# Norm roots moved behind the products: query, key and last-gate rows of a two-block network on one core

## The reference, cut to what matters

```
# h: 256 x 1024 after the state-space mixer
h = h + sigmoid(rms_norm(h, ple_norm[0]) @ gate_w[0]) * (p[0] @ proj_w[0])
k, v = split(rms_norm(h, kv_norm) @ kv_w)            # 256 + 256 columns
k = rope(rms_norm(k per head of 64, k_norm))
q, gate = split(rms_norm(h, attn_norm) @ in_w)       # 1024 + 1024 columns
q = rope(rms_norm(q per head of 64, q_norm))
h = h + (attention(q, k, v, window 128, sinks) * silu(gate)) @ out_w
h = h + sigmoid(rms_norm(h, ple_norm[1]) @ gate_w[1]) * (p[1] @ proj_w[1])
rms_norm(x, w) = x / sqrt(mean(x*x) + 1e-6) * w
```

## Time and profile before

| | |
|---|---|
| median of 3 runs | 924.22 us (922.49 to 926.22) |
| the profiled execution, its own time | 927.82 us |
| its span in the profile | 926.0 us |
| PE busy | 887.0 us (96%) |
| DVE busy | 667.6 us (72%) |
| ACT busy | 512.7 us (55%) |
| TensorE clock granted, mean | 0.988 of full speed |

### The profile page before, as it was taken

One profiled execution on the slowest core, in us unless ns is written; L12 is line 12 of the kernel. 1 busy time (PEld: TensorE's weight loads), 2 busy tenths in 40 slices (PEclk: granted clock), 3 DMA queues, 4 the chain that ended last, 5 costly groups with the idle time before them and its releaser, 6 DMA issues.

```text
span 926.0 us, 13925 instructions
## 1 busy us (share of the span) xinstructions
PE 887.0 (96%) x5463; PEld 771.8 (83%) x5463; DVE 667.6 (72%) x971; ACT 512.7 (55%) x742; POOL 73.4 (8%) x79
## 2 busy tenths in 40 slices
PE   6999899899999989999999899999999998999998
PEld 6997788788888779999988699988888886878777
DVE  6688648928677688888844687796786777776665
ACT  6865424235453566666534565854756566576553
POOL 6001213100000000000000000007220000000000
PEclk9999999999999999999999999999999998999999
DMA  9542242124554466556555356544223444522231
GB/s 303 173 137 92 92 119 91 46 90 154 196 176 148 170 211 199 183 190 202 201 181 182 104 175 196 169 137 137 92 92 107 178 159 155 197 92 91 92 120 62
DMA packets 80977, 136.37 MB, mean 147 GB/s; under 512 B 3957, under 2 KB 46545, under 8 KB 80912
## 3 DMA queue, kind: packets, MB, share of 16 engines
q1 hardware_dynamic: 78800, 130.95, 43.0%
q0 software_dynamic: 2112, 4.53, 1.8%
HBM read 134.42 MB, written 1.05 MB: 146 GB/s over the span
## 4 chain that ended last, share of the span: by engine, by line
PE 66%; ACT 5%; DVE 5%; issue 3%; DMA 2%; DVEq 0%; ACTq 0%
PE bank L449 19%; PE bank L450 18%; PE bank L451 18%; PE bank L438 3%; DVE lower L1930 2%; ACT upper L1345 1%; PE bank L1124 1%; PE bank L929 1%; PE bank L937 1%; DMA loaded<-in_ssm_in_w 1%; PE bank L1108 1%; ACT arena L1444 1%; ACT arena L1846 1%; DMA loaded<-in_ple_gate_w 1%; DMA loaded<-in_ffn_w_up 1%
## 5 line engine op out<-in xcount | busy, mean ns | idle before, releaser
L1930 DVE TENSOR_TENSOR lower<-loaded,upper 128x2048 fp32r<-128x2048 f32 x122 | 280.7, 2304 | 131.5 <-ACT upper L1345 129.7
L1345 ACT ACTIVATE upper<-loaded 128x2048 fp32r<-128x2048 f32 x122 | 231.9, 1904 | 116.4 <-PE bank L451 97.2
L449 PE MATMUL bank<-xT_upper,upper 128*128 128x256 f32 (+1 forms) x664 | 187.8, 283 | 1.2 <-DVE xT_lower L1995 1.2
L450 PE MATMUL bank<-xT_lower,upper 128*128 128x256 f32 (+1 forms) x664 | 186.1, 280 | 0.0
L451 PE MATMUL bank<-xT_upper,lower 128*128 128x256 f32 (+1 forms) x664 | 186.1, 280 | 0.0
L449 PE MATMUL bank<-upper,xT_upper 128*128 128x512 f32 (+1 forms) x360 | 145.7, 405 | 5.9 <-DVE lower L1930 3.5
L451 PE MATMUL bank<-upper,xT_lower 128*128 128x512 f32 (+1 forms) x360 | 140.3, 390 | 0.0
L450 PE MATMUL bank<-lower,xT_upper 128*128 128x512 f32 (+1 forms) x360 | 139.6, 388 | 0.0
L449 PEld LDWEIGHTS bank<-xT_upper,upper 128*128 128x128 f32 (+1 forms) x664 | 126.3, 190 | 2.3 <-issue 2.1
L451 PEld LDWEIGHTS bank<-xT_upper,lower 128*128 128x128 f32 (+1 forms) x664 | 126.6, 191 | 0.1
L450 PEld LDWEIGHTS bank<-xT_lower,upper 128*128 128x128 f32 (+1 forms) x664 | 126.4, 190 | 0.1
(11 more groups left out here) (344 smaller groups left out, 1101.2 us busy)
## 6 DMA issues: line engine op xcount, KB each, us to landing
loaded<-in_w_in SPq DMA_DIRECT2D x26, 1024.0 KB, 5.2
loaded<-in_ffn_w_up SPq DMA_DIRECT2D x22, 1024.0 KB, 5.1
loaded<-in_ssm_in_w SPq DMA_DIRECT2D x20, 1024.0 KB, 5.3
loaded<-in_ffn_w_down SPq DMA_DIRECT2D x11, 1024.0 KB, 5.0
loaded<-in_ssm_out_w SPq DMA_DIRECT2D x8, 1024.0 KB, 4.9
loaded<-in_ple_gate_w SPq DMA_DIRECT2D x8, 1024.0 KB, 5.2
loaded<-in_attn_in_w SPq DMA_DIRECT2D x8, 1024.0 KB, 5.1
loaded<-in_w_branch_ret SPq DMA_DIRECT2D x4, 1024.0 KB, 5.0
```

The lines of the kernel that those rows point to most:

```text
L449: mm(out, a[0], b[0], start=start, stop=False)
L450: mm(out, a[0], b[1], start=False, stop=False)
L1345: A(part(upper, PARTS, n), part(loaded, LOADS, n), ACT.Copy).then_inc(uppers, 1)
L1930: TT(part(lower, LOADS, n), part(loaded, LOADS, n), part(upper, PARTS, n).bitcast(F32), sub) \
```

## The change

Norm 4 and norm 5 are no longer applied to the rows before these are turned. PE turns the plain rows of h (`plain_turns`); the norm's weights (one per column of h) go on in the turned blocks as before; and the row's factor 1/root, one number per row, goes on after the product: as the scale of ACT's operation that reads the product (squares of the heads, value rows, the SiLU and sigmoid gates), and as a factor in `rs8` for keys and queries. `late_root` on DVE takes the reciprocals. The sums for norm 4 move behind `norm_upper(4, xT, (1,))` on ACT and those of norm 5 behind the split of `pg10.1`'s weights. Two units, `pg10.0` and `pg10.1`, get places of their own in the arena: their loads wait for earlier events, the upper part of `pg10.0` too, and its split moves ahead of `softmax_out(11)`.

```diff
+        OWN = [index["pg10.0"], index["pg10.1"]]
 
         def part(of, slots, n):
             nk, width = units[n][3], units[n][5]
+            if of is upper and n == OWN[0]:
+                return ar(13312, SLOT, of=split_arena)
+            if of is not upper and n in OWN:
+                return ar((5120, 23552)[OWN.index(n)], SLOT) if of is loaded else own_lower[OWN.index(n)][:, :]
...
         def part_free(eng, n):
 
-            if n >= PARTS:
+            if n == OWN[0]:
+                emptied(eng, ("aqT", 0, 1), ("aqT", 1, 1))
+            elif n >= PARTS:
                 eng.wait_ge(*unit_done[n - PARTS])
...
+            def plain_turns(n, i, halves=(0, 1)):
+
+
+                for key, bank, k0, m in pieces(n, i):
+                    if (k0 + m > 4) in halves:
+                        if n == 4:
+                            pe.wait_ge(sem("ple_joined"), i + (3 if k0 + m > 4 else 1))
+                        else:
+                            pe.wait_ge(sem("h_ready"), 9 + i)
+                        turns(key, bank, [h[:, i, P * k:P * k + P] for k in range(k0, k0 + m)])
...
-                                 lambda blocks: xT_ready(n, blocks), None)
+                                 lambda blocks: xT_ready(n, blocks), (lambda: plain_turns(4, 0, (0,))) if f else None)
 
             embed(0)
 
-            norm_turns(4, (0,))
+            plain_turns(4, 0, (1,))
+            plain_turns(4, 1, (0,))
             rows_by_tile("kv", [("kv", i) for i in range(2)], (2, 3), xT2,
-                         lambda blocks: pe.wait_ge(sem("xT2_lower_ready"), blocks), lambda: norm_turns(4, (1,)))
+                         lambda blocks: pe.wait_ge(sem("xT2_lower_ready"), blocks), lambda: plain_turns(4, 1, (1,)))
...
-            out_turns(1, 1, 0)
+            out_turns(1, 1, 7)
             embedding_product(1, 1, 0)
-            ao_tile(4, 1)
-            ao_tile(5, 1)
-            norm_turns(5, (0,))
-            ao_tile(6, 1)
-            ao_tile(7, 1)
-            embedding_product(1, 1, 1)
+            plain_turns(5, 0)
+            for t in range(4, 8):
+                ao_tile(t, 1)
...
             gate_piece(0, 0, 0, 0)
+            embedding_product(1, 1, 1)
             gate_piece(0, 1, 0, 0)
-            norm_turns(5, (1,))
+            plain_turns(5, 1)
...
-                if n >= LOADS:
+                if n == OWN[0]:
+                    sp.wait_ge(sem("hn_in"), 2)
+                elif n == OWN[1]:
+                    emptied(sp, ("kv", 0), ("kv", 1))
+                elif n >= LOADS:
                     sp.wait_ge(*unit_done[n - LOADS])
...
                         if f == 0:
                             split_to(f"pg{m}0.1", 1 + i)
-                            if m == 0 and i:
-                                first_sums(0)
-                        elif m == 0 and i == 0:
-                            first_sums(1)
-                            root_table()
-                            other_sums(0)
+                        elif i == 0:
+                            columns_upper(4, xT2, "kv_norm_w_2", 0, 0, 2)
                             split_to("pg01.1", 1)
-                            columns_upper(4, xT2, "kv_norm_w_2", 0)
 
             embed(0)
-            root_table()
-            other_sums(1)
-            norm_upper(4, xT, (0,))
+            columns_upper(4, xT2, "kv_norm_w_2", 0, 2, 4)
             columns_upper(4, xT2, "kv_norm_w_2", 1)
             split_to("pg01.1", 2)
+            norm_upper(4, xT, (0,))
             split_to("ain0.1", -1)
             norm_upper(4, xT, (1,))
+            root_table()
+            for i in range(2):
+                first_sums(i)
+                other_sums(i)
...
-                A(sq, ps[:, 0:width], ACT.Square).then_inc(sem("hn_sq"), 1)
+                A(sq, ps[:, 0:width], ACT.Square, scale=rstd[:, key[-1]:key[-1] + 1]).then_inc(sem("hn_sq"), 1)
...
+            act.wait_ge(sem("late_root"), 2)
             for i in range(2):
                 head_squares(asq[:, i, 512:768], ("kv", i), 256)
                 ps = full(act, ("kv", i))
-                A(vv[:, i, :, 0:64], ps[:, 256:512].rearrange("p (a b) -> p a b", a=4), ACT.Copy).then_inc(sem("v_rows"), 1)
+                A(vv[:, i, :, 0:64], ps[:, 256:512].rearrange("p (a b) -> p a b", a=4), ACT.Identity,
+                  scale=rstd[:, i:i + 1]).then_inc(sem("v_rows"), 1)
...
-            root_table()
+            split_to("ao3", 1)
             upper_of(aoT, ("aoT", 1, 1), 4, 1)
-            row_sums(5, 0)
-            split_to("ao3", 1)
             norm_upper(5, xT, (0,))
             split_to("ao3", 2)
+            root_table()
+            row_sums(5, 0)
             row_sums(5, 1)
             split_to("pg10.1")
             norm_upper(5, xT, (1,))
...
+            def late_root(n, i):
+
+
+                ve.wait_ge(sem("root"), 2 * n + i + 1)
+                ve.reciprocal(rstd[:, i:i + 1], rstd[:, i:i + 1]).then_inc(sem("late_root"), 1)
...
             embed(0)
-            ve.wait_ge(sem("xT2_lower_ready"), 8)
-            scale(4, 0, xT, "attn_norm_w_2")
-            row_scale(4, 1)
-            lower_rows(4, 0, xT)
+            columns_lower(4, xT2, "kv_norm_w_2", 0, 2, 4)
             columns_lower(4, xT2, "kv_norm_w_2", 1)
             split_to("pg01.1", 2)
             ve.wait_ge(sem("xT2_lower_ready"), 16)
+            scale(4, 0, xT, "attn_norm_w_2")
+            lower_rows(4, 0, xT)
             split_to("ain0.1", -1)
             scale(4, 1, xT, "attn_norm_w_2")
             lower_rows(4, 1, xT)
+            for i in range(2):
+                late_root(4, i)
...
                 link(ve.reciprocal(rs8[:, :, heads_], rs8[:, :, heads_]))
+                n = heads_.stop - heads_.start
+                link(TT(rs8[:, :, heads_], rs8[:, :, heads_], bc(rstd[:, 0:2].unsqueeze(2), P, 2, n), mul))
...
+            split_to("ao3", 1)
             softmax_out(11)
             gate(1, 1, 11)
             plain_join("fo", 0)
             lower_of(aoT, ("aoT", 1, 1), 4, 1)
-            row_scale(5, 0)
             scale(5, 0, xT, "ple_norm_w_2", 8)
-            split_to("ao3", 1)
             lower_rows(5, 0, xT)
             plain_join("fo", 1)
             split_to("ao3", 2)
-            row_scale(5, 1)
             split_to("pg10.1")
             scale(5, 1, xT, "ple_norm_w_2", 8)
             lower_rows(5, 1, xT)
+            for i in range(2):
+                late_root(5, i)
```

More of the change, by code:

```diff
@@ L196, in build @@
         split_arena = nc.alloc_sbuf_tensor_at("split_arena", [P, ARENA], F32R, offset=arena_at)
+        own_lower = [nc.alloc_sbuf_tensor_at(f"own_lower{m}", [P, SLOT], F32R, offset=arena_at + 4 * at)
+                     for m, at in enumerate((5120, 23552))]
         PS = [ctx.enter_context(nc.psum_tensor(f"bank{b}", [P, 512], F32)) for b in range(8)]
@@ L1036, in embed @@
             def embed(m):
-                n = 3 if m == 0 else 5
+                n = 3
                 norm_turns(n, (0,))
[L1039 to L1043, removed]
+                for f in range(2):
+                    for i in range(2):
+                        embedding_product(0, f, i)
+                norm_turns(n, (1,))
                 for f in range(2):
                     rows_by_tile(f"pg{m}{f}", [("pg", m, f, i) for i in range(2)], (2 * f, 2 * f + 1), xT,
-                                 lambda blocks: xT_ready(n, blocks), None)
+                                 lambda blocks: xT_ready(n, blocks), (lambda: plain_turns(4, 0, (0,))) if f else None)
             embed(0)
-            norm_turns(4, (0,))
+            plain_turns(4, 0, (1,))
+            plain_turns(4, 1, (0,))
             rows_by_tile("kv", [("kv", i) for i in range(2)], (2, 3), xT2,
-                         lambda blocks: pe.wait_ge(sem("xT2_lower_ready"), blocks), lambda: norm_turns(4, (1,)))
+                         lambda blocks: pe.wait_ge(sem("xT2_lower_ready"), blocks), lambda: plain_turns(4, 1, (1,)))
             AIN = ((0, 1), (2, 3), (0, 1), (2, 3))
@@ L1385, in row_sums @@
                     act.wait_ge(sem("h_ready"), 2 * n + i - 1)
-                A(dump if n in (1, 2) else hs[:, i, :], h[:, i, :], ACT.Square, accum_out=ssq[:, i:i + 1]) \
+                A(dump if n in (1, 2, 5) else hs[:, i, :], h[:, i, :], ACT.Square, accum_out=ssq[:, i:i + 1]) \
                     .then_inc(sem("sq_done"), 1)
@@ L1394, in first_sums @@
                 act.wait_ge(sem("ple_joined"), i + 1)
-                A(hs[:, i, 0:512], h[:, i, 0:512], ACT.Square, accum_out=ssq[:, 2 + i:3 + i]).then_inc(sem("sq_first"), 1)
+                A(dump[:, 0:512], h[:, i, 0:512], ACT.Square, accum_out=ssq[:, 2 + i:3 + i]).then_inc(sem("sq_first"), 1)
                 act.wait_ge(sem("sq_first"), i + 1)
@@ L1401, in other_sums @@
                 act.wait_ge(sem("h_ready"), 7 + i)
-                A(hs[:, i, 512:D], h[:, i, 512:D], ACT.Square, accum_out=ssq[:, i:i + 1]).then_inc(sem("sq_done"), 1)
```

(17 more changed lines are left out.)

2 lines of the change are left out of this document (removed).

## The result

The changed kernel takes 933.51 us in the median of 4 runs (933.45 to 936.05), the kernel before 925.0 us (4 runs, 922.49 to 926.22): ratio 1.0097, 95% interval 1.007 to 1.0123. Run again beside the kernel before, it took 934.12 us against 926.36, ratio 1.0087 (1.0059 to 1.0114). It is slower by about 0.9%, 8 us. The forecast was 931.2 us.

The account below looks back on a forecast made before the run. PE, busy 96% of the span, was taken to bound the kernel, so gains come only from its idle or low-clock stretches. 2.2 + 2.3 + 2.5 = 7.0 us on the 924.2 us median gave 931.2 us, range 922.5 to 935.5.

Parts of the forecast that it names:

- Norm 4, +2.2 us forecast: Query product after norm 4: PE waits 2.7, 0.3 and 6.1 us, so ain1 starts at 796.7, not 794.5: +2.2 us.
- the signs: First gate to end of kv: no idle PE and a clock of 1.0 there would show the forecast right.
- the cause that I named: At ain1: norm 4's sums and late root in ACT's in-order list delay the split and key rows; PE stands 6.1 us.
- The clock, +2.3 us: Behind the 6.1 us wait at ain1: PE's clock falls to 1.2 GHz, costing +2.3 us.
- the middle of two seen prices, 1.7 and 2.9: Earlier clock falls: 1.7 us behind a 4.47 us wait, 2.9 us at kv tile 1; the forecast took 2.3.
- The last gate, +2.5 us: Last gate: PE waits 1.7, 0.4 and 2.4 us, starting pg11.0's piece at 908.15, before at 905.74: +2.5 us.
- The first of the two causes: Last gate, DVE: softmax_out(11) stands behind the lower part of pg10.0, a new PE wait of 1.7 us.
- The other: Last gate, ACT: pg11.0's upper part comes only after the root's table and two row sums; PE waits 2.4 us.
- The late roots do not hold PE: Norm 4: sums slip into ACT's idle time, ain1 follows ain0; norm 4 gives -3.9, total 922.8 us; chance 0.13.
- Same waits, no extra low clock: Whole change: the forecast waits without another clock fall, +4.7 us, 928.9 us; chance 0.15.
- only the last gate is misjudged: Last gate: softmax_out(11) is not held up, +0.8 in place of +2.5 us, 929.5 us; chance 0.10.
- The clock falls at the last gate as well: Last gate: its three close waits bring one more fall, 1.7 to 2.9 us, about 933.5 us; chance 0.15.

Follow-up runs that it names:

- n4_only: The changed kernel with only its norm 4 part; norm 5 and the last gate as in the kernel before: 932.65 us, ratio 1.0066 to before.
- sums4_early: The changed kernel, but ACT makes the sums of norm 4 in its idle time and the late roots follow at once: 927.84 us, ratio 1.0013 to before.
- busy_wait: The changed kernel plus 24 matrix instructions on PE ahead of ain1, writing a bank nobody reads: 934.05 us, ratio 1.0079 to before.
- n5_only: The changed kernel with only its norm 5 and last gate part; norm 4 as in the kernel before: 928.07 us, ratio 1.0026 to before.
- gate_split_early: The changed kernel, but pg10.0 is split earlier on ACT and DVE, in unit z = 11: 930.91 us, ratio 1.0074 to before.
- sums5_moved: The changed kernel, but ACT's root table and norm 5 tile 0 sums precede pg10.1's split, tile 1's follow the last upper parts: 933.68 us, ratio 1.0098.
- all_three: The changed kernel with the edits of sums4_early, gate_split_early and sums5_moved together: 925.0 us, ratio 0.9996 to before.

## Why the prediction was right, point by point

- **Norm 4, +2.2 us forecast.** From the mark to `ain1`: 794.49 - 746.97 = 47.5 us before, 795.14 - 745.28 = 49.9 after, +2.3. The wait at `ain1` was given as 6.1 us and is 5.7 idle (5.9 if it is counted at the pitch of 0.23 us, as the forecast did); the two before it as 2.7 and 0.3, and are 1.97 and 0.74. PE has no idle time between the first gate and the end of `kv`, and the clock is 1.00 there, as the signs asked. n4_only and sums4_early show the cause that I named.
- **The clock, +2.3 us.** `ain1` takes 2.4 us longer. busy_wait shows that the 2.4 us of this stage are separate from the wait, though the end of the kernel did not gain them. That the middle of two seen prices, 1.7 and 2.9, came within 0.2 us is luck; only the two bounds had a reason. The fall of before at 775 us did go, as forecast; its 3.1 us are not a gain on top, since they were inside the 794.5.
- **The last gate, +2.5 us.** n5_only measures it alone: +2.48. The first of the two causes is confirmed by gate_split_early, -1.7 us. The other was only half of the story: with the sums out of the way the load of `pg11.0` holds PE, 1.0 us earlier than the sums did. The three waits, given as 1.7, 0.4 and 2.4 us, are 1.50, 0.19 and 2.14.
- **Missed, +0.2 us.** The gates' SiLU is scaled per row too, and I had left that operation out. Two of them stand between two table loads on ACT and take 1.27 us where they took 1.09. The first such pair (828.55 to 831.13 us) does not hold PE. Behind the second (852.70 to 855.28) PE waits 0.29 us at 858.72, where before it waited 0.12, and from there on it is 4.97 us later than before, counted from the mark, where it had been 4.80.
- **The sum.** 7.0 us forecast, 7.49 from mark to end, 7.8 and 8.5 between the medians. The measured 933.5 lies in the wide range (922.5 to 935.5) and 0.5 us above the one that the forecast gave for itself (929.5 to 933). The profiled executions differ by less, 5.7 us, because the mark came 1.7 us earlier in that of the changed kernel, ahead of all that was changed. The 2.3 us by which 933.5 exceeds 931.2 are 0.5 us of the sum, 0.8 us by which the median of before rose with one more run, and about 1 us that stays open. Without low clock the tails differ by 8.0 us; if the kernel before falls at 775 us in only some executions, the medians would lie apart by more than the two profiles show. No run measured how often it does.
- **Rivals.** "The late roots do not hold PE" was brought about by sums4_early: from the mark to `ain1` it takes 44.2 us, 3.3 less than before, where that rival reckoned 3.9. Its median is still 2.3 us above before (ratio 1.0013, 0.9993 to 1.0032) and not 1.4 below, and its tail is only 0.6 us shorter, as the waits ahead of `ain0` and at the last gate remain. "Same waits, no extra low clock" falls with the low clock at `ain1`, "only the last gate is misjudged" with the 1.50 us wait of `softmax_out(11)`. "The clock falls at the last gate as well" gave 933.5, the number that was measured, but in the profiled execution of 933.56 us the clock did not fall there; in that of the change again (933.91) it did, at 911 to 915 us, which cost 1.7 us. So that agreement of numbers is chance, and the fall at the last gate comes in some executions only.

## What to carry to other kernels

Moving an operation off one chain puts it on another: price the list it is moved into, with all that stands behind it (here 5.3 us of table load and sums ahead of a split and of the keys' rows, both of which PE needed), not only the wait that it leaves. Look for the engine's own idle stretches first; the same work cost 8 us of the tail at one place in ACT's list and a wait of 0.3 us at another. And repair waits one at a time, asking each time what comes last next: of the edits here one handed half of its wait on to a load, and one all of it to the keys' columns.

## What the runs showed of the hardware

- The wait of 5.7 us at `ain1` was followed by the lower clock in all five profiles that have it (the change twice, gate_split_early, sums5_moved, n4_only); the wait filled with work was not. Waits of 2.0 and 0.7 us close together left it alone in sums4_early and all_three; those of 1.36 and 1.26 us of the kernel before were followed by it in both profiles that have them (before and n5_only). At the last gate, with the same waits of 1.5, 0.2 and 2.1 us, it fell in busy_wait and in the change's second profile, and not in its first and in n5_only. The same program thus runs with different falls.
- The times of one kernel spread by up to 9 us (before: 922.38 to 931.37 in 25 runs). The falls are not shown to be the whole cause: the longest of these runs has a mean granted clock of 0.991, and so has the median one, 925.54.
- A per-row scale on ACT costs 0.09 us: the squares and value rows of 128x256 are 0.47 us long here and 0.37 to 0.40 before, and the last gate's sigmoid of 512 columns 0.69 against 0.60.
- The Trainium skill (ScalarE: Activation LUTs, section "What ACT_TABLE_LOAD costs") gives about 93 ns for each such per-row operand; the trace agrees, with 0.09 us. Its drain of 1.38 us at a switch of tables does not show: the load at 782.75 ends at 784.03 and the next operation starts at 784.04.
